# Reordering the weight splits, lows and queries of a two-block transformer kernel

## What is computed

```python
def second_block(x, mem, ...):
    h = rmsnorm_2(x, norm_mix_g[l])
    x = x + hybrid_mixer(h, w_in[l], ..., w_out[l], slopes)
    h = rmsnorm_2(x, norm_xattn_g[l])
    x = x + memory_cross_attention(h, rmsnorm_2(mem, norm_mem_g[l]), xattn_wq[l], xattn_wkv[l], xattn_wo[l])
    h = rmsnorm_2(x, norm_ffn_g[l])
    x = x + conv_ffn(h, ffn_w_up[l], ..., ffn_w_down[l])
    return rmsnorm_2(x, final_norm_g)

def memory_cross_attention(h, mem_n, wq, wkv, wo):
    q = (h @ wq).reshape(Bsz, T, N_XATTN_HEADS, HEAD_DIM)
    k, v = jnp.split(mem_n @ wkv, 2, axis=-1)
    ...
    p = jax.nn.softmax(s, axis=-1).astype(v.dtype)
    o = jnp.einsum('bhtm,bmhd->bthd', p, v).reshape(Bsz, T, XATTN_WIDTH)
    return o @ wo
```

## Time and profile before

| | us |
|---|---|
| median of 3 runs | 1504.49 |
| lowest, highest | 1504.47, 1505.58 |
| the profiled execution, its own time | 1505.2 |
| its span (first to last instruction) | 1503.5 |
| PE busy in it | 1433.4 |
| DVE, ACT, POOL busy in it | 1090.5, 837.4, 360.5 |

### The profile page before, as it was taken

The page is one execution under the profiler, slowest core; times in us unless marked ns, Lnnn a source line. Parts: engine busy times, 40 slices in busy tenths (PEclk is TensorE's granted clock), DMA queues, the critical chain, the costliest instruction groups (busy, mean ns, idle before and its releaser), DMA issues.

```text
span 1503.5 us, 25899 instructions
## 1 busy us (share of the span) xinstructions
PE 1433.4 (95%) x10424; PEld 1329.3 (88%) x10424; DVE 1090.5 (73%) x1904; ACT 837.4 (56%) x1441; POOL 360.5 (24%) x222
## 2 busy tenths in 40 slices
PE   4998999899999999999999999999998999799997
PEld 3988978899999999999988888887888889799997
DVE  6678778656779888899756666677667557698752
ACT  3444764544454677777645444555455656576651
POOL 2222100233345200000122332344243111232210
PEclk9999999999999999999999999999999999999999
DMA  9747856455555544444457666666675435276530
GB/s 366 245 146 226 275 173 217 147 169 167 181 185 169 182 141 150 146 144 152 142 169 223 193 196 191 218 184 192 194 262 185 135 98 169 85 225 190 188 113 29
DMA packets 74009, 269.29 MB, mean 179 GB/s; under 512 B 8433, under 2 KB 9762, under 8 KB 73122
## 3 DMA queue, kind: packets, MB, share of 16 engines
q1 hardware_dynamic: 71568, 257.46, 54.2%
q10 hardware_dynamic: 1426, 7.56, 1.4%
q0 software_dynamic: 896, 2.62, 0.5%
HBM read 263.93 MB, written 3.67 MB: 178 GB/s over the span
## 4 chain that ended last, share of the span: by engine, by line
PE 82%; DVE 9%; ACT 5%; issue 1%; DMA 1%; POOL 1%; SPq 0%; DVEq 0%; ACTq 0%
PE bank L600 81%; DVE split L1767 2%; ACT split L1248 1%; DVE PR L2205 1%; DVE ada_acc L1804 1%; DMA xT<-in_xT 1%; DVE PR L2202 1%; DMA far<-in_w_ada 1%; DVE rT L1847 0%; POOL split L2541 0%; POOL sc_g L2635 0%; PE bank L768 0%; DVE PR L2210 0%; DVE H L2296 0%; ACT PA L1362 0%
## 5 line engine op out<-in xcount | busy, mean ns | idle before, releaser
L600 PE MATMUL bank<-H,split 128*128 128x256 f32 x5976 | 750.6, 286 | 19.7 <-DVE split L1767 5.4
L600 PEld LDWEIGHTS bank<-H,split 128*128 128x128 f32 x5976 | 728.8, 193 | 26.8 <-issue 13.6
L1248 ACT CAST split<-ringb 128x1024 fp32r<-128x1024 f32 x350 | 365.6, 1046 | 281.9 <-PE bank L600 276.2
L600 PE MATMUL bank<-split,H 128*128 128x512 f32 (+1 forms) x1728 | 391.4, 388 | 5.3 <-POOL split L2541 2.0
L1767 DVE TENSOR_TENSOR split<-ringb,split 128x1024 fp32r<-128x1024 f32 x258 | 327.1, 1270 | 89.9 <-ACT split L1248 89.7
L2541 POOL TENSOR_TENSOR split<-ringb,split 128x1024 fp32r<-128x1024 f32 x92 | 229.2, 2491 | 668.5 <-ACT split L1248 668.5
L600 PEld LDWEIGHTS bank<-split,H 128*128 128x128 f32 x1728 | 321.7, 188 | 73.1 <-issue 4.0
L2296 DVE TENSOR_TENSOR H<-PR,H 128x256 fp32r<-128x256 f32 x128 | 133.5, 1045 | 108.2 <-ACT H L1581 108.2
L1767 DVE TENSOR_TENSOR split<-far,split 128x1024 fp32r<-128x1024 f32 x79 | 105.7, 1346 | 55.1 <-ACT split L1248 55.1
L1248 ACT CAST split<-far 128x1024 fp32r<-128x1024 f32 x91 | 94.8, 1046 | 63.9 <-PE bank L600 59.3
L2555 POOL TENSOR_TENSOR rT<-rT 128x256 f32<-128x256 f32 x25 | 25.1, 1005 | 200.7 <-ACT rT L1297 199.1
(11 more groups left out here) (292 smaller groups left out, 1274.8 us busy)
## 6 DMA issues: line engine op xcount, KB each, us to landing
ringb<-in_u SPq DMA_DIRECT2D x128, 512.0 KB, 3.8
ringb<-in_v SPq DMA_DIRECT2D x128, 512.0 KB, 4.4
ringb<-in_w_ada SPq DMA_DIRECT2D x28, 512.0 KB, 5.1
far<-in_w_up SPq DMA_DIRECT2D x27, 512.0 KB, 4.5
far<-in_w_ada SPq DMA_DIRECT2D x20, 512.0 KB, 5.5
ringb<-in_w_up SPq DMA_DIRECT2D x17, 512.0 KB, 4.5
ringb<-in_w_pq SPq DMA_DIRECT2D x16, 512.0 KB, 4.3
far<-in_w_dn SPq DMA_DIRECT2D x14, 512.0 KB, 3.9
```

The source lines that it names most:

```text
L600: return TE.matmul(o, l, r, start=start, stop=stop, skip_group_check=True)
L1248: S.copy(buf(m)[0], slots[P.slot[m]]).then_inc(hi_done, 1)
```

## The change

1. `Plan.buffers` takes the order of a new ring from an argument: new buffers that are `free` (buffer 7) come first, then the known ones by last use, then the newest, then the other new ones.
2. From `w2_xl` to the last `w2_xo` the ring has six buffers, 0, 1, 2, 7, 3, 4, and from `w_up` on seven, with 5 in addition; buffer 6 is no longer used. The lead is 4 for `w2_xl` and `w2_xq` 0, 5 up to `w_up`, then 6 as before. By the plan xv1, xo0, xo1, up0 now have buffers 3, 4, 2, 0 (before 2, 0, 7, 3) and are due at xl0, xq0, xq1, xq1 (before xq0, xq1, xv0, xv0).
3. On ACT the casts of up1, up2 and up3 stand between the later steps of the attention to the memory, none between the tiles of `w2_xo`. On DVE the lows due at `w2_xv` and the first `w2_xo` stand ahead of the attention's last steps, those of the second `w2_xo` behind the residuals, and the low of up4 is no longer ahead of `root(5)` but behind the normalised tiles. The `lows_ahead()` between the two `w2_xq` blocks are gone.
4. On PE one step of `memory_values` comes ahead of the scores, and one less behind them. `w2_mk` has `alone=4`.
5. DVE takes the two query blocks of `w2_mq` out one by one: block 0 behind the first four scaled tiles, block 1 behind the last four. The low of mk0 comes ahead of the scaled tiles, that of mk1 behind query block 0.
6. The lows of `fn`'s tiles come one residual pair earlier where they can: low 0 behind pair 0, lows 1 and 2 behind pair 1, 3 and 4 behind pair 2, 5 to 7 behind pair 3.

```diff
--- before.py
+++ after.py
@@ -106,7 +106,7 @@
             uses[s] = self.use[i] = uses.get(s, 0) + 1
             last[s] = i
 
-    def buffers(self, ring_of, lead_of, late):
+    def buffers(self, ring_of, lead_of, late, free):
         n = len(self.units)
         self.buf, self.buf_prev = [None] * n, [None] * n
         self.hi_no, self.raw_no = [0] * n, [0] * n
@@ -125,7 +125,8 @@
 
                 known = sorted((x for x in ring if x in before and x != newest), key=last.get)
                 new = [x for x in ring if x not in before]
-                order[ring] = new[:2] + known + new[2:] + [x for x in ring if x == newest]
+                order[ring] = ([x for x in new if x in free] + known + [x for x in ring if x == newest]
+                               + [x for x in new if x not in free])
                 before = ring
             k = at.get(ring, 0)
             at[ring] = k + 1
@@ -219,15 +220,16 @@
     P.slots({"far": range(7), "four": range(4), "far2": list(range(7, 13)) + list(range(4))})
     PQ0, U0, PA0, UP0, QI0 = P.at["w_pq", 0], P.at["u", 0], P.at["w_pa", 0], P.at["w_up", 0], P.at["w_qi", 0]
     XK0 = P.at["w2_xk", 0]
-    ring4, ring3, ring3x, ring7 = tuple(range(4)), tuple(range(3)), (0, 1, 2, 7), tuple(range(7))
+    XL0 = P.at["w2_xl", 0]
+    ring4, ring3, ring3x, ring6, ring7 = tuple(range(4)), tuple(range(3)), (0, 1, 2, 7), (0, 1, 2, 7, 3, 4), (0, 1, 2, 7, 3, 4, 5)
 
     def ring_of(i):
-        return ring7 if i >= UP0 else ring3x if i >= XK0 else ring3 if i >= PA0 else ring4
+        return ring7 if i >= UP0 else ring6 if i >= XL0 else ring3x if i >= XK0 else ring3 if i >= PA0 else ring4
 
     def lead_of(i):
-        return 0 if i < QI0 - 1 else 3 if i < PA0 else 2 if i < XK0 - 2 else 3 if i < UP0 - 4 else 5 if i < UP0 else 6
-
-    P.buffers(ring_of, lead_of, {QI0 + 2: QI0 + 1})
+        return 0 if i < QI0 - 1 else 3 if i < PA0 else 2 if i < XK0 - 2 else 3 if i < XL0 else 4 if i < XL0 + 2 else 5 if i < UP0 else 6
+
+    P.buffers(ring_of, lead_of, {QI0 + 2: QI0 + 1}, (7,))
     first = [P.at[nm, j] for nm in ("w_pq", "w2_xq") for j in range(2)] + list(range(UP0, UP0 + 4))
     O0, DN6 = P.at["w2_o", 0], P.at["w_dn", 6]
 
@@ -472,12 +474,13 @@
 
         slots = [ringb[:, i, :] for i in range(4)] + [far[:, i, :] for i in range(3)] + [far2[:, i, :] for i in range(6)]
         bufs = [(split[:, i, 0, :], split[:, i, 1, :]) for i in range(3)]
-        bufs1 = bufs + [(split1[:, 0, 0, :], split1[:, 0, 1, :])] + 3 * [None] + [(split5[:, 0, :], split5[:, 1, :])]
-        bufs2 = bufs + [(split4[:, i, 0, :], split4[:, i, 1, :]) for i in range(4)]
-        UP0 = P.at["w_up", 0]
+        last_buf = [(split5[:, 0, :], split5[:, 1, :])]
+        bufs1 = bufs + [(split1[:, 0, 0, :], split1[:, 0, 1, :])] + 3 * [None] + last_buf
+        bufs2 = bufs + [(split4[:, i, 0, :], split4[:, i, 1, :]) for i in range(4)] + last_buf
+        XL0 = P.at["w2_xl", 0]
 
         def buf(n):
-            return (bufs2 if n >= UP0 else bufs1)[P.buf[n]]
+            return (bufs2 if n >= XL0 else bufs1)[P.buf[n]]
 
         VO = A["voff"]
 
@@ -1094,7 +1097,7 @@
 
             lin("w2_mq", 4, of(Ym), lambda k: t.wait_ge(un_lo, k + 1), begin=1)
             mh = normed(3)
-            lin("w2_mk", 4, hk, mh, both=True, alone=2)
+            lin("w2_mk", 4, hk, mh, both=True, alone=4)
             lin_nat("w2_mv", hkt, mh, 512)
 
             def need_m():
@@ -1202,9 +1205,10 @@
                 t.wait_ge(*evac("w2_xl", 0))
 
             values = memory_values()
+            fill(values, 1)
             work = attend(ATT_X, need_x, lambda: t.wait_ge(*evac("w2_xv", 0)))
             next(work)
-            fill(values, 5)
+            fill(values, 4)
             next(work)
             next(work)
             fill(values, 3)
@@ -1241,10 +1245,10 @@
                     s.wait_ge(slot_in[P.slot[m]], 16 * P.use[m])
                     if P.buf_prev[m] is not None:
                         s.wait_ge(pe_done, P.unit_no[P.buf_prev[m]])
-                    if m >= UP0 and P.buf[m] >= 3:
+                    if P.buf[m] == 7:
+                        s.wait_ge(c_lo, 128)
+                    elif m >= XL0 and P.buf[m] >= 3:
                         s.wait_ge(ev_v, EV["w2_o" if P.buf[m] < 5 else "w2_xo", 3][1])
-                    elif P.buf[m] == 7:
-                        s.wait_ge(c_lo, 128)
                     S.copy(buf(m)[0], slots[P.slot[m]]).then_inc(hi_done, 1)
                 st["pos"] += 1
 
@@ -1701,18 +1705,17 @@
             root(4)
             copy_out("w2_xl", 0, xkT[:, T:2 * T], T)
             units("w2_xq", 2)
-            unit("w2_xv")
             work = attend(ATT_X, lambda: None)
             for _ in range(4):
                 next(work)
             copy_out("w2_xv", 0, xv)
+            for name in ("w2_xv", "w2_xv", "w2_xo"):
+                unit(name)
+                next(work)
             for _ in work:
                 pass
             root_table()
-            unit("w2_xv")
             for c in range(4):
-                if c == 2:
-                    unit("w2_xo")
                 for i in (2 * c, 2 * c + 1):
                     s.wait_ge(ev_v, EV["w2_xo", c][1] - 1 + i % 2)
                     high(5, i)
@@ -2313,9 +2316,8 @@
                 v.wait_ge(fn_t, d + 1)
                 v.wait_ge(x_re, 16)
                 residual("fn", d, banks[bank_of["fn", d]], 40)
-                if d:
-                    low(3, (2 * d - 2, 2 * d - 1))
-            low(3, (6, 7))
+                low(3, range(max(2 * d - 1, 0), 2 * d + 1))
+            low(3, (7,))
             for i in range(2):
 
                 v.wait_ge(sq_done, 8 * 3 + 6 + 2 * i)
@@ -2327,17 +2329,21 @@
             V.scalar_tensor_tensor(out=mean(3), in0=banks[7][:, 0:T], scalar=EPS, in1=s2, op0=ALU.mult, op1=ALU.add).then_inc(z_done, 1)
             root(3)
             scaled = norm_steps(3, xT, lambda j: gfm[:, j:j + 1])
+            unit("w2_mq")
             for _ in range(4):
                 next(scaled)
             V.tensor_copy(s2, recip(3)).then_inc(r_kept, 1)
-            unit("w2_mq")
+
+            def take_queries(p):
+                v.wait_ge(r_kept, 1)
+                V.tensor_tensor(tri3(mqT[:, p * 512:(p + 1) * 512], 2), tri3(take_out("w2_mq", p), 2),
+                                s2.rearrange("p (a t) -> p a t", a=1).broadcast_to((128, 2, T)), ALU.mult).then_inc(ev_v, 1)
+
+            take_queries(0)
             lows_ahead()
             for _ in scaled:
                 pass
-            v.wait_ge(r_kept, 1)
-            for p in range(2):
-                V.tensor_tensor(tri3(mqT[:, p * 512:(p + 1) * 512], 2), tri3(take_out("w2_mq", p), 2),
-                                s2.rearrange("p (a t) -> p a t", a=1).broadcast_to((128, 2, T)), ALU.mult).then_inc(ev_v, 1)
+            take_queries(1)
 
 
             def keep_steps():
@@ -2462,23 +2468,20 @@
             root(4)
             for j in range(2):
                 unit("w2_xq")
-                lows_ahead()
                 V.tensor_tensor(xqT[:, j * T:(j + 1) * T], take_out("w2_xq", j)[:, 0:T], recip(4), ALU.mult).then_inc(ev_v, 1)
-            unit("w2_xv")
             work = attend(ATT_X, lambda: None)
             for _ in range(5):
                 next(work)
-            unit("w2_xv")
+            units("w2_xv", 2)
+            unit("w2_xo")
             for _ in work:
                 pass
             for c in range(4):
-                if c % 2 == 0:
-                    unit("w2_xo")
                 residual("w2_xo", c, take_out("w2_xo", c))
                 if c:
                     low(5, (2 * c - 2, 2 * c - 1))
             low(5, (6, 7))
-            lows_ahead()
+            unit("w2_xo")
             root(5)
             scaled = norm_steps(5, xT, lambda j: vec("norm_ffn_g", j))
             for _ in range(4):
```

## The result

The changed kernel takes 1497.91 us (median of 6 runs, 1495.97 to 1500.52) where the kernel before takes 1505.28 on the same chip: a ratio of 0.9953, 95% interval 0.9940 to 0.9967. (One of the six executions of the kernel before took 7916.43 us; the ratio leaves it out.) Faster, as forecast, but by 7.4 us and not by 11.5. Its profiled execution took 1500.52, with a span of 1498.8.

The account below looks back on a forecast made before the run. PE was taken as the bound, busy 1433.4 of 1503.5 us, so only its waits and half clock pay. −3.1 (with part one's +0.6) and −8.5 made −11.6 us from median 1504.49: forecast 1493.0, range 1490.5 to 1498.0.

Parts of the forecast that it names:

- the last term of part three: `w_up` behind its first `H` product: PE follows POOL at 0.83 us a tile, −0.6 us.
- costed at nothing: Feed-forward start: DVE enters 1.8 us more behind, covered by about 4 us in hand; 1.8 us at most without cover.
- Part one: Lows between the residuals of `fn`: one more low ahead of PE's first `Ym` product, a loss of 0.6 us.
- Part two: Mixer's queries ahead of half the scaled tiles: 2.85 us wait and half clock go; stage −3.1 us, including +0.6.
- Part three: Six buffers round the attention to the memory: stage −8.5 us, −8.0 of it between `w2_xo` and `H`.
- ACT and PE keep step: `w2_xo` residuals: ACT 1.5 to 1.6 us a pair, PE 1.43 a block; PE's sums start at 8.5 us.
- hand-offs: Attention-to-memory stage: ten hand-offs in a chain, timed only one at a time, +0.5 us.
- Rival A: Ahead of `Ym`: clock falls in the widened 1.7 us gap, costing 1.5 us: 1494.5; chance 0.22.
- Rival B: `w2_mk`: POOL's and DVE's lows block each other, mk1 or tile 3 2 us late, clock falls: 1496.4; chance 0.10.
- Rival C: Behind `w2_xo`'s last residual: squares and sums bind, PE 3 us later, clock lost (1.4): 1497.4; chance 0.13.
- D: Whole kernel: no effect, since another wait ends last everywhere: 1504.5; chance 0.02.
- E: Feed-forward part: DVE becomes the bound, kernel slower; 1515 with 20 lows slowed by 2.2 us each; chance 0.03.

Follow-up runs that it names:

- the changed kernel's first and third profile: The full change against the kernel before, run and profiled, then repeated word for word: first 1497.91 us (0.9953), third 1496.25 us (0.9929).
- part two alone: Kernel before plus only `alone=4`, mk0's low ahead of the scaled tiles, first query block ahead of the second four: 1504.23 us, ratio 0.9989.
- the second of the changed kernel: The changed kernel repeated word for word against the kernel before: 1497.75 us, ratio 0.9948.
- alone=2: The changed kernel with `alone=2` in place of 4 for `w2_mk`: 1496.58 us, ratio 0.9930 to the kernel before.

## Why the prediction was wrong, and where it was right

The size was wrong: 7.4 us were gained in the median where 11.5 were forecast, and 1497.91 lies 0.1 us inside the upper end of the range. By the marks the stages gave −9.2 where −11.6 were forecast. The direction of every part, the waits that went and the order of the three by size were right. The step that failed most is the last term of part three: that POOL would make the tiles of `H` at 0.83 us each, and that the unit lows moved behind the norm could be costed at nothing. The runs show three lows of units on DVE meeting POOL's lows of `H`, where there had been one, and each meeting lengthens one tile by 1.0 us. Step by step:

**Part one, +0.6 forecast, +1.14 measured.** The term was mis-sized. The queue was counted about rightly (0.48 and 0.19 us in the trace), and 0.43 of the rest is the meeting with POOL's sum of squares, which the experiment that held POOL back took away. I had priced the low by rows in which POOL was idle, and the move had pushed it under POOL's work.

**Part two, −3.1 with part one's 0.6, measured −2.90 and −0.66 beside the +1.14.** Right to 0.2 us. The 2.85 us went. Of the 1.4 for the clock 0.7 came back in the step behind. The 0.5 us that PE was to wait for mk1 and for tile 3 do not show as a wait in the changed kernel's first and third profile, and as one of 0.39 in its second. But the 96 products with `H` take 12.43 us there, where 96 at 0.1195 are 11.5: by this estimate 0.9 us of stops too short to be listed are left, behind POOL's tiles, and the 0.5 was too low.

**Part three, −8.5 forecast, −6.8 measured.** The 0.5 ahead of the scores gave 0.73. From `w2_xo` to `H` 13.9 were forecast, 14.87 measured. The step that failed is "ACT and PE keep step": PE's sums start at 9.57 us (1298.29 less 1288.72) and not at 8.5, and the waits of 0.26, 0.44 and 0.26 us before them name DVE. Behind the sums 5.30 us pass, where 5.4 were forecast. DVE's lows of `MH` stand beside POOL's sums of squares here too, in the changed kernel:

```profile
1293.62 3.87 POOL L2558 TENSOR_TENSOR rT<-rT 128x256 f32<-128x256 f32 x4 [0.40 <-ACT rT L1301]
...
1294.50 1.35 DVE L1866 SCALAR_TENSOR_TENSOR MH<-xT,vecs,MH 128x256 fp32r<-128x256 f32 x2
```

1.35 for two in place of 0.86. That this is all of the 1.0 us wasn't tried, so its cause stays open.

The larger miss is the block behind `H`: −0.6 forecast, +0.96 measured, 1.56 us. Two steps of the text met here. The lows of up4 and up5 were "costed at nothing", with the 4 us that the units have in hand as cover. That cover held: PE never waited for a unit's low. But the lows took POOL's time. The 0.83 a tile had been taken from between two rows, 2.83 us for four tiles with no low beside them and 4.81 beside two. These rows already held the price, 2.0 us for two lows, and it goes by the low and not by the tile. Three lows meet POOL's eight tiles in the changed kernel, where one did before: 8.64 and 6.61 us. I had asked who waits for the moved low, and not whom it makes wait. With the low of up4 elsewhere (that of up5 stays beside POOL) one low meets it, POOL takes 6.63 to 6.64 again and the step is 1.89 shorter, in three profiles.

Added up: 0.54 + 0.19 − 0.33 + 0.97 + 1.56, less the 0.5 us of hand-offs that had been put into the sum, is 2.4, which is 11.6 − 9.2.

**Rival A (the clock falls in the gap that part one widens), 0.22.** The mechanism is real. Of seven profiles with part one, the six with the gap of 2.29 us split evenly: the clock stayed at 1.00 in three and fell in three (the seventh, with 1.85, kept it). The gap of 1.14 us, where part one is left out, never lost it. PE in the third profile of the changed kernel, and its window of 3 us (PE busy, PEld, DVE, ACT, POOL, clock, DMA share, GB/s):

```profile
1128.81 3.88 PE L603 MATMUL bank<-Ym,split 128*128 128x256 f32 x18 [2.29 <-DVE xT L1880]
```

```profile
1128.80:1131.80 3.00, 2.99 (x15) 3.00 (x16) 3.00 (x9) 2.95 (x9) 0.00 (x0) 0.56 0.04 15
```

18 products take 3.88 us in place of 2.36, and the step to `H` 18.15 in place of 16.62: 1.53, the price that was given. The gap was larger than the 1.7 us I had weighed. The Trainium skill (TensorE: Matmul & The Clock Gate, section "What's actually happening") says of the start of a kernel that the moment of the change depends on the phase in which work meets the gate, and differs between runs of one kernel. These profiles show the like in the middle of one: 3 against 3 behind one and the same gap of 2.29 us, and 4 against 10 behind the gap of 1.82 at 769 us. So the length of such a gap alone doesn't say whether the clock falls. An estimate of part one's price from these six profiles is 1.14 plus half of 1.53. Six are few for a share, and the three that lost the clock are those whose mark came earliest (1121.35 to 1121.87, against 1123.21 and later); whether that is chance no run tells.

**Rival B** fell: no wait of its 2 us took the place of the one removed. Its mechanism shows small in three profiles, as waits for POOL of 0.73 us (part two alone), 0.39 (the second of the changed kernel) and 0.24 (`alone=2`). **Rival C** (squares and sums bind behind the last residual) was partly right: the chain does bind there, by 1.07 us and not 3, through DVE's lows and not ACT's squares, and the clock stayed at 1.00. **D** fell. **E** fell: lows of over 3 us on DVE do appear in the feed-forward part, and PE waits for none of them.

**Median and span.** The forecast was made from 1504.49 us, and the kernel before gave 1505.28 in the comparison itself and 1505.34 to 1506.98 in the later ones. Its own 16 runs put the changed kernel at 1496.7 (medians of 1497.91, 1497.75 and 1496.25), some 8.8 below the 1505.5 that most of these are near. The three comparisons gave 7.4, 7.6 and 10.7 us one by one. So the 9.2 of the stages (7.7 where the clock falls, rival A) fits the medians, with the toss of the first 1120 us around it; more than that they don't show.

## What to carry to other kernels

Before moving an operation into a gap, look at who works beside it on a resource that both need, in both directions: whether the neighbour makes the moved one longer (part one, 0.43 us), and whether the moved one makes the neighbour longer that PE is waiting for (up4's low, 1.9 us). Count the meetings, 1.0 us each here, and not an average pace. The best place for an operation of DVE is a stretch in which POOL is idle and DVE waits for something else; up4's low in DVE's wait for the sums cost nothing and brought 1.9 us. And when a result of a few tenths of a per cent doesn't fit the stages, cut both traces at marks ahead of the change and behind it, and profile both kernels again, before the change is blamed for the rest.

## What was new about the hardware

- VectorE and GpSimd block each other by whole instructions. A low on DVE of 1.21 us took 3.43 when POOL's record began 0.03 us earlier, and POOL's of 2.37 took 3.49 when it began 0.01 us earlier and DVE won. The Trainium skill (SBUF — State Buffer, section "SBUF: two separate sides") describes such an exclusive lock; the rows agree on the blocking (the record that starts first isn't always the winner), and the stakes are new: PE's 2.28 us wait and its clock hang on some hundredths of a microsecond.
- The blocking shows in rows of short operations as well: a tile of `H` takes POOL 0.75 us, and 1.73 to 1.77 when it meets a unit's low on DVE, one tile for each low. Two lows of DVE that take 0.86 us take 1.34 beside POOL's sum of squares.
- The same gap of 2.29 us, behind the same work, was followed by full clock in three profiles and by half in three; one of 1.82 us by full clock in ten and by half in four.
- Executions of one kernel differ by 6.3 us at 1120 us, most of it in discrete steps: 2.7 to 3.1 us at the start, 3.7 at 497 us, 1.6 at 769. Medians of five or six runs of the changed kernel lie between 1496.25 and 1497.91.
